# Loading two of 336 expert slabs by eight-partition transfers on eight DMA engines

## The chip, the cores and the metric

One core of one Trainium2 chip runs the kernel. The metric is the time of one execution on the device in microseconds. What reads as "the clock" below is the share of TensorE's full clock that was granted.

## What is computed

The reference is a trunk of two layers on 256 tokens of width 1024, with a memory of 256 rows. Each layer has a mixer (stick-breaking attention, chunked gated linear attention and cross attention to the memory, each gated and summed). The first layer then has a dense SwiGLU block, the second a mixture of experts:

```python
def moe_swiglu(h, w_router, w_gate_up, w_down):
    t = h.reshape(-1, dm)
    top_val, top_idx = lax.top_k((t @ w_router), TOP_K)          # 2 of 8 experts
    top_w = jax.nn.softmax(top_val, axis=-1)
    combine = jnp.sum(jax.nn.one_hot(top_idx, N_EXPERTS) * top_w[..., None], axis=1)
    for e in range(N_EXPERTS):
        y = y + combine[:, e:e + 1] * swiglu(t, w_gate_up[e], w_down[e])
```

An expert's weights are 1024 x 7168 (gate and up) and 3584 x 1024 (down), in float32. All eight experts are used, so 352 MB of expert weights pass through the core in one execution.

## The kernel before

The mixers and the dense block run first, to about 735 us. The change touches only what comes after: the mixture of experts, and how its weights are loaded.

**Slots and slabs.** The experts are worked on in slots, one expert a slot and eight of them here (an expert with too many tokens would get a slot more). A slot takes 96 tokens in three blocks of 32, or 64 in two blocks; `BLOCKS_AT` (line 80) gives the first seven as 3, 2, 3, 2, 3, 3, 2, and the eighth has two. An expert's weights come as 42 slabs of 128 partitions x 2048 floats, 1 MB each (`EXP_SLABS`, line 57), 336 slabs in all. On the host they are laid out as `moe_slabs[expert, j // 3, partition, j % 3, :]`, so that three slabs in a row are 24 KB of contiguous memory in each partition (`expert_slabs_in_order`, line 2388). Inside a slot PE works the slabs off in order: gate and up of 1024 hidden columns, the next gate and up, then the down product of the columns before, and so on. The last six slabs (36 to 41) are down products, with the gathering of the next slot's tokens between slabs 37 and 38.

**Buffers.** `exp_raw` (line 234) holds 21 slabs; slab j of a slot from the third one on lies in place j % 21. The first two slots use one more buffer, exp_extra, and load each slab by a transfer of its own (`single_slabs`, line 592). From the third slot on, `expert_slabs` (line 603) loads slabs 0 to 38 of a slot by 13 transfers of three slabs (line 610), and slabs 39, 40 and 41 by single ones (line 616). All are issued by SP, in the order of use. Before each one SP waits for `slab_used`, which PE raises after its last matmul on a slab, so that a place is free before it is loaded again. SP's program has the third slot written out and the others as a loop over i, from 3 to the number of slots (lines 648 to 652). The number of the expert is read from a table at each slot.

**Waits of PE.** `wait_slab` (line 372): PE waits for `more_ready` at each third slab and for one of three `end_ready` semaphores at each of the last three. A landed transfer adds 16. PE, ScalarE and VectorE have slots 0 to 6 written out, and then a loop.

Of the kernel before, what the change touches and what calls it, by code (L numbers as in the profile page):

```python
# [13 lines left out]
P = 128  # L14
# [10 lines left out]
D_FF, EXPERTS, D_EXP = 2816, 8, 3584  # L25
# [15 lines left out]
EXP_RAW, LOAD = 21, 3  # L41
FIRST_RAW = EXP_RAW + 1
SINGLE_SLOTS = 2
DGE_SCRATCH = 4096


# [10 lines left out]
EXP_SLABS = sum(GU) + sum(DN)  # L57
SINGLE = SINGLE_SLOTS * EXP_SLABS
HT = DM // P
# [20 lines left out]
BLOCKS_AT = (3, 2, 3, 2, 3, 3, 2)  # L80
# [87 lines left out]
def trunk(nc, x_in, mem_in, mix_norm_g, w_in, sb_q_g, sb_k_g, gla_a_up, gla_a_b, gla_o_g, ca_q_g,  # L168
# [10 lines left out]
    with ExitStack() as ctx:  # L179
        def sb(name, shape, dt=F32):  # L180
            return ctx.enter_context(nc.sbuf_tensor(name, shape, dt))

        def sem(name):
            return ctx.enter_context(nc.semaphore(name))
# [14 lines left out]
        slot_i = sb("slot_i", [1, 1 + EXPERTS + OVER], I32)  # L199
# [34 lines left out]
        exp_raw = sb("exp_raw", [P, EXP_RAW, EXP_SLAB])  # L234
# [121 lines left out]
        more_ready = [sem(f"more_ready{i}") for i in range(EXP_RAW // LOAD)]  # L356
        end_ready = [sem(f"end_ready{i}") for i in range(LOAD)]

        END = EXP_SLABS - LOAD

        def load_ready(i, j):

            if j % EXP_RAW == END % EXP_RAW:
                return i * 16
            return i * (16 * EXP_SLABS // EXP_RAW) + 16 * (j // EXP_RAW)

        def place(i, j):

            n = i * EXP_SLABS + j if type(i) is int else SINGLE
            return n % FIRST_RAW if n < SINGLE else j % EXP_RAW  # L370

        def wait_slab(pe, i, j):

            if type(i) is int and i * EXP_SLABS + j < SINGLE:
                pe.wait_ge(first_ready[place(i, j)], 16 * ((i * EXP_SLABS + j) // FIRST_RAW + 1))
            elif j >= END:
                pe.wait_ge(end_ready[j - END], i * 16 + 16)
            elif j % LOAD == 0:
                pe.wait_ge(more_ready[j % EXP_RAW // LOAD], load_ready(i, j))
# [176 lines left out]
        def _(sp):  # L556
# [35 lines left out]
            def single_slabs(e, i, js):  # L592
                for j in js:
                    sp.wait_ge(slab_used, i * EXP_SLABS + (PRE + j + 1 - FIRST_RAW))
                    sp.dma_start(exp_slots[place(i, j)], moe_slabs[bass.ds(e, 1), j // LOAD, :, j % LOAD, :]
                                 .rearrange("e p n -> (e p) n"))\
                        .then_inc(first_ready[place(i, j)], 16)

            def last_holder(j):

                return max(n for n in range(SINGLE) if n % FIRST_RAW == j)

            def expert_slabs(e, i):
                for j in range(0, END, LOAD):
                    if type(i) is int and j < EXP_RAW:
                        sp.wait_ge(slab_used, PRE + 1 + max(last_holder(j + n) for n in range(LOAD)))
                    else:
                        sp.wait_ge(slab_used, i * EXP_SLABS + (PRE + j + LOAD - EXP_RAW))
                    n = j % EXP_RAW
                    sp.dma_start(exp_raw[:, n:n + LOAD, :].rearrange("p a n -> p (a n)"),  # L610
                                 moe_slabs[bass.ds(e, 1), j // LOAD]
                                 .rearrange("e p a n -> (e p) (a n)"))\
                        .then_inc(more_ready[n // LOAD], 16)
                for j in range(END, EXP_SLABS):
                    sp.wait_ge(slab_used, i * EXP_SLABS + (PRE + j + 1 - EXP_RAW))
                    sp.dma_start(exp_slots[j % EXP_RAW], moe_slabs[bass.ds(e, 1), j // LOAD, :, j % LOAD, :]
                                 .rearrange("e p n -> (e p) n"))\
                        .then_inc(end_ready[j - END], 16)

# [19 lines left out]
            for n in range(EXP_RAW // LOAD):  # L639
                sp.sem_inc(more_ready[n], load_ready(SINGLE_SLOTS, n * LOAD) - 16)  # L640
            for n in range(LOAD):
                sp.sem_inc(end_ready[n], SINGLE_SLOTS * 16)
            single_slabs(0, 0, range(FIRST_RAW, EXP_SLABS))
            sp.wait_ge(r_table, 1)
            slots = sp.value_load(slot_i[0:1, 0:1], min_val=EXPERTS, max_val=SLOTS)
            e = sp.value_load(slot_i[0:1, 2:3], min_val=0, max_val=EXPERTS - 1)
            single_slabs(e, 1, range(EXP_SLABS))
            e = sp.value_load(slot_i[0:1, 3:4], min_val=0, max_val=EXPERTS - 1)
            expert_slabs(e, SINGLE_SLOTS)
            with sp.Fori(SINGLE_SLOTS + 1, slots) as i:  # L650
                e = sp.value_load(slot_i[0:1, bass.ds(i + 1, 1)], min_val=0, max_val=EXPERTS - 1)
                expert_slabs(e, i)
            for t in range(NT):
# [1165 lines left out]
        def _(pe):  # L1819
# [478 lines left out]
            def expert(i, blocks, blocks_ago, blocks_next):  # L2298
                j = 0

                def gate_and_up(s, part):
                    nonlocal j
                    w = 2 * lanes_wide(s)
                    n = KT // GU[s]
                    for q in part:
                        wait_slab(pe, i, j)
                        for kk in range(n):
                            k = q * n + kk
                            if is_first(i) and (s, k) == (0, KT // 2):
                                pe.wait_ge(x_dve, 1)  # L2310
                            for b in range(blocks):
                                for g in range(LANES):
                                    c = kk * LANES * w + g * w
                                    ins = mm(lane(pa, g)[:, b * BW:b * BW + w],
                                             xf[:, k, b * LANE:(b + 1) * LANE],
                                             exp_slots[place(i, j)][:, c:c + w],
                                             k == 0, k == KT - 1)
                        ins.then_inc(slab_used, 1)
                        j += 1

                def down(s, part):
                    nonlocal j
                    pe.wait_ge(e_turned, i * STEPS + (s + 1))
                    chunks = hidden_chunks(s)
                    n = EXP_SLAB // DM
                    for q in part:
                        wait_slab(pe, i, j)
                        for kk in range(n):
                            k = q * n + kk
                            for b in range(blocks):  # L2330
                                for g in range(LANES):
                                    c = kk * DM + g * OUT
                                    ins = mm(lane(ps, g)[:, b * OUT:(b + 1) * OUT],
                                             hf[:, s % 2, (b * chunks + k) * LANE:
                                                (b * chunks + k + 1) * LANE],
                                             exp_slots[place(i, j)][:, c:c + OUT],
                                             s == 0 and k == 0 and b * OUT % BW == 0,
                                             s == STEPS - 1 and k == HT_END - 1)
                        ins.then_inc(slab_used, 1)
                        j += 1  # L2340
# [101 lines left out]
```

## Time and profile before

| what | value |
|---|---|
| median of 3 runs | 1557.95 us (1557.13 to 1558.28) |
| the profiled execution | 1556.87 us |
| its span, first to last instruction | 1555.1 us |
| granted TensorE clock | 0.995 |
| PE, VectorE, ScalarE, GpSimd busy | 97%, 35%, 28%, 5% |
| moved by DMA | 480.50 MB, mean 309 GB/s |

The span is the time between the first and the last instruction of the profiled execution; the 1.8 us between it and the time of that execution lie around it. Busy shares are means over the whole span. The DMA share is the mean over the core's sixteen DMA engines, so that a share of one half can mean sixteen engines at half their time or eight engines at all of theirs. A number behind `x` is a count.

### The profile page before, as it was taken

What the parts mean: (1) busy time and instruction counts of PE and PEld (TensorE: products, weight loads), DVE (VectorE), ACT (ScalarE), POOL (GpSimd) and SP (SyncE); (2) the same over time, 40 slices, a digit from 0 to 9 for tenths busy, and PEclk for the clock granted to TensorE, in tenths of its full rate; (3) what the DMA queues carried; (4) which work ended last, traced back from release to release, by engine and by line L of the source; (5) the groups of instructions that cost most, each with busy time, mean ns of one, the idle gap of its engine ahead of it and who ended that gap; (6) DMA issues with size and microseconds to landing.
All of it is one profiled execution on the core that took longest, in us unless ns stands there. A gap on an engine that the chain in (4) does not pass through costs nothing.

```text
span 1555.1 us, 33054 instructions
## 1 busy us (share of the span) xinstructions
PE 1505.2 (97%) x15014; PEld 972.0 (63%) x15014; DVE 544.1 (35%) x638; ACT 439.9 (28%) x566; POOL 81.1 (5%) x117
## 2 busy tenths in 40 slices
PE   8999999999999999999999999999999999999876
PEld 6888888788888887888335353354543553545324
DVE  5755575655567664666200101001010010010100
ACT  5557654544445657453000000000000000000000
POOL 5211100000002111000000000000000000000000
PEclk9999999999999999999999999999999999999999
DMA  7555454665655654777999999999999999999995
GB/s 274 178 155 169 141 172 155 224 189 175 204 177 177 189 151 149 247 274 278 420 421 392 415 427 428 425 430 427 427 428 428 428 427 427 414 418 425 428 429 220
DMA packets 86361, 480.50 MB, mean 309 GB/s; under 512 B 10384, under 2 KB 12496, under 8 KB 63184
## 3 DMA queue, kind: packets, MB, share of 16 engines
q1 hardware_dynamic: 84592, 474.67, 78.6%
q0 software_dynamic: 1632, 3.74, 0.8%
q8 instruction: 118, 1.93, 0.5%
q14 instruction: 19, 0.16, 0.0%
HBM read 477.34 MB, written 1.05 MB: 308 GB/s over the span
## 4 chain that ended last, share of the span: by engine, by line
PE 87%; DMA 7%; DVE 2%; POOL 2%; issue 1%; ACT 0%; SPq 0%; DVEq 0%; POOLq 0%
PE pa L2045 28%; PE ps L2045 20%; PE pa L1916 13%; PE pa L1918 12%; PE pa L1917 12%; DMA exp_raw<-in_moe_slabs 6%; DVE w_lo L1240 1%; DMA w_raw<-in_w_mem_kv 1%; POOL hrs L763 1%; POOL head_gains L692 0%; PE ps L1843 0%; PE ps L2218 0%; PE ps L2039 0%; DVE hs L1788 0%; PE pa L1951 0%
## 5 line engine op out<-in xcount | busy, mean ns | idle before, releaser
L2045 PE MATMUL pa<-exp_raw,xf 128*32 128x512 f32 (+1 forms) x5064 | 490.8, 542 | 15.9 <-DMA exp_raw<-in_moe_slabs 12.8
L2045 PEld LDWEIGHTS pa<-exp_raw,xf 128*32 128x32 f32 x5064 | 176.2, 110 | 306.1 <-issue 232.8
L1240 DVE TENSOR_TENSOR w_lo<-w_raw,w_hi 128x1024 fp32r<-128x1024 f32 x226 | 274.2, 1231 | 121.9 <-ACT w_hi L876 113.0
L876 ACT ACTIVATE w_hi<-w_raw 128x1024 fp32r<-128x1024 f32 (+1 forms) x228 | 236.9, 1053 | 148.6 <-PE pa L1918 147.2
L2045 PE MATMUL ps<-exp_raw,hf 128*32 128x256 f32 x4480 | 251.8, 379 | 14.6 <-issue 8.4
L1916 PE MATMUL pa<-w_hi,r 128*128 128x512 f32 x600 | 240.5, 401 | 1.9 <-DVE r L1275 1.8
L1917 PE MATMUL pa<-w_lo,r 128*128 128x512 f32 x600 | 234.6, 391 | 0.0
L1918 PE MATMUL pa<-w_hi,r 128*128 128x512 f32 x600 | 234.5, 391 | 0.0
L2045 PEld LDWEIGHTS ps<-exp_raw,hf 128*32 128x32 f32 x4480 | 152.9, 110 | 112.9 <-issue 22.2
L1788 DVE TENSOR_TENSOR hs<-pa,hs 128x768 f32<-128x768 f32 (+3 forms) x32 | 23.7, 741 | 569.3 <-ACT hs L1195 569.3
L1195 ACT ACTIVATE hs<-pa 128x768 f32<-128x768 f32 (+3 forms) x32 | 20.4, 637 | 588.7 <-PE pa L2045 588.7
L1916 PEld LDWEIGHTS pa<-w_hi,r 128*128 128x128 f32 x600 | 112.9, 188 | 29.4 <-issue 3.2
L1918 PEld LDWEIGHTS pa<-w_hi,r 128*128 128x128 f32 x600 | 113.0, 188 | 24.4
L1917 PEld LDWEIGHTS pa<-w_lo,r 128*128 128x128 f32 x600 | 113.2, 189 | 22.1
L1916 PE MATMUL pa<-w_hi,xt 128*128 128x512 f32 (+1 forms) x320 | 123.3, 385 | 2.9 <-DVE xt L1275 2.7
L1918 PE MATMUL pa<-w_hi,xt 128*128 128x512 f32 (+1 forms) x320 | 121.3, 379 | 0.0
L1917 PE MATMUL pa<-w_lo,xt 128*128 128x512 f32 (+1 forms) x320 | 121.3, 379 | 0.0
L1916 PEld LDWEIGHTS pa<-w_hi,xt 128*128 128x128 f32 x320 | 60.2, 188 | 16.0 <-issue 2.7
L1918 PEld LDWEIGHTS pa<-w_hi,xt 128*128 128x128 f32 x320 | 60.2, 188 | 11.5
L1917 PEld LDWEIGHTS pa<-w_lo,xt 128*128 128x128 f32 x320 | 60.2, 188 | 10.6
L1773 DVE TENSOR_TENSOR yf<-ps,yf 128x768 fp32r<-128x768 f32 (+1 forms) x7 | 5.9, 843 | 75.9 <-ACT yf L1182 75.9
L1182 ACT ACTIVATE yf<-ps 128x768 fp32r<-128x768 f32 (+1 forms) x7 | 5.0, 719 | 82.7 <-PE ps L2045 82.7
(266 smaller groups left out, 831.6 us busy)
## 6 DMA issues: line engine op xcount, KB each, us to landing
exp_raw<-in_moe_slabs SPq DMA_DIRECT2D x78, 3072.0 KB, 28.7
exp_raw<-in_moe_slabs SPq DMA_DIRECT2D x99, 1024.0 KB, 10.0
w_raw<-in_w_in SPq DMA_DIRECT2D x104, 512.0 KB, 4.4
w_raw<-in_ff_w_gate_up SPq DMA_DIRECT2D x44, 512.0 KB, 4.6
w_raw<-in_ff_w_down SPq DMA_DIRECT2D x22, 512.0 KB, 4.2
w_raw<-in_w_mem_kv SPq DMA_DIRECT2D x16, 512.0 KB, 5.6
w_raw<-in_w_out SPq DMA_DIRECT2D x16, 512.0 KB, 4.4
w_raw<-in_w_br_sb SPq DMA_DIRECT2D x8, 512.0 KB, 3.8
```

The source lines that it names most:

```text
L763: pool.tensor_tensor(dst[:, 0:n], src[:, 0:n], half[:, 0:n], ALU.pow)\
L876: act.activation(dst, raw, ACT.Copy).then_inc(hi_ready, 1)
L1182: act.activation(yf[:, 0, 0:blocks * OUT], ps[:, 0:blocks * OUT], ACT.Copy)\
L1195: act.activation(hidden_rows(s, blocks), gate_up(s, 0, blocks), ACT.Silu)\
L1240: dve.tensor_tensor(dst, raw, hi.bitcast(F32), ALU.subtract)\
L1773: dve.tensor_tensor(yf[:, 1, 0:blocks * OUT], ps[:, 0:blocks * OUT], yf[:, 0, 0:blocks * OUT].bitcast(F32), ALU.subtract)\
L1788: dve.tensor_tensor(hidden_rows(s, blocks), gate_up(s, 1, blocks), hidden_rows(s, blocks), ALU.mult).then_inc(e_h, 1)
L1916: pe.matmul(dst, hi, m_hi, start=first, stop=False)
L1917: pe.matmul(dst, hi, m_lo, start=False, stop=False)
L1918: return pe.matmul(dst, lo, m_hi, start=False, stop=last)
L2045: return pe.matmul(dst, a, b, start=start, stop=stop, skip_group_check=True)
```

## The change

In the slots with i = 3 and i = 5 (`LOW_SLOTS`), slab 41, the last one, is no longer loaded by one transfer of 128 partitions. It is loaded by sixteen transfers of eight partitions each, with 8 KB a partition. `LOW_SETS` lists them: for k = 0 to 3 and a = 0 to 3, the partitions 32k + a, 32k + a + 4, ... up to 32k + a + 28. Each adds 16 to a semaphore of their own, `low_ready`, and PE waits for 256 of it a set. As these slots no longer raise `end_ready[2]`, the later waits on that semaphore are lower by 16 for each such slot before. To tell the slots apart, SP's loop is written out for slots 2 to 6 (`range(SINGLE_SLOTS, len(BLOCKS_AT))`) and remains a loop from slot 7 on. The first condition in `expert_slabs` gains `i == SINGLE_SLOTS`, so that only the third slot takes its waits from the buffers' first holders, as before.

```diff
--- before.py
+++ after.py
@@ -41,6 +41,8 @@
 EXP_RAW, LOAD = 21, 3
 FIRST_RAW = EXP_RAW + 1
 SINGLE_SLOTS = 2
+LOW_SLOTS = (3, 5)
+LOW_ROWS, LOW_STEP = 8, 4
 DGE_SCRATCH = 4096
 
 
@@ -356,7 +358,16 @@
         more_ready = [sem(f"more_ready{i}") for i in range(EXP_RAW // LOAD)]
         end_ready = [sem(f"end_ready{i}") for i in range(LOAD)]
 
+        low_ready = sem("low_ready")
+
         END = EXP_SLABS - LOAD
+        LAST = EXP_SLABS - 1
+        LOW_SETS = [slice(32 * k + a, 32 * (k + 1), LOW_STEP)
+                    for k in range(P // 32) for a in range(LOW_STEP)]
+
+        def low_before(i):
+
+            return sum(n < i for n in LOW_SLOTS) if type(i) is int else len(LOW_SLOTS)
 
         def load_ready(i, j):
 
@@ -373,6 +384,10 @@
 
             if type(i) is int and i * EXP_SLABS + j < SINGLE:
                 pe.wait_ge(first_ready[place(i, j)], 16 * ((i * EXP_SLABS + j) // FIRST_RAW + 1))
+            elif j == LAST and type(i) is int and i in LOW_SLOTS:
+                pe.wait_ge(low_ready, 16 * len(LOW_SETS) * (low_before(i) + 1))
+            elif j == LAST:
+                pe.wait_ge(end_ready[j - END], i * 16 + 16 * (1 - low_before(i)))
             elif j >= END:
                 pe.wait_ge(end_ready[j - END], i * 16 + 16)
             elif j % LOAD == 0:
@@ -602,7 +617,7 @@
 
             def expert_slabs(e, i):
                 for j in range(0, END, LOAD):
-                    if type(i) is int and j < EXP_RAW:
+                    if type(i) is int and i == SINGLE_SLOTS and j < EXP_RAW:
                         sp.wait_ge(slab_used, PRE + 1 + max(last_holder(j + n) for n in range(LOAD)))
                     else:
                         sp.wait_ge(slab_used, i * EXP_SLABS + (PRE + j + LOAD - EXP_RAW))
@@ -613,6 +628,13 @@
                         .then_inc(more_ready[n // LOAD], 16)
                 for j in range(END, EXP_SLABS):
                     sp.wait_ge(slab_used, i * EXP_SLABS + (PRE + j + 1 - EXP_RAW))
+                    if j == LAST and type(i) is int and i in LOW_SLOTS:
+                        for rows in LOW_SETS:
+                            sp.dma_start(exp_raw[rows, j % EXP_RAW, :],
+                                         moe_slabs[bass.ds(e, 1), j // LOAD, rows, j % LOAD, :]
+                                         .rearrange("e p n -> (e p) n"))\
+                                .then_inc(low_ready, 16)
+                        continue
                     sp.dma_start(exp_slots[j % EXP_RAW], moe_slabs[bass.ds(e, 1), j // LOAD, :, j % LOAD, :]
                                  .rearrange("e p n -> (e p) n"))\
                         .then_inc(end_ready[j - END], 16)
@@ -645,9 +667,10 @@
             slots = sp.value_load(slot_i[0:1, 0:1], min_val=EXPERTS, max_val=SLOTS)
             e = sp.value_load(slot_i[0:1, 2:3], min_val=0, max_val=EXPERTS - 1)
             single_slabs(e, 1, range(EXP_SLABS))
-            e = sp.value_load(slot_i[0:1, 3:4], min_val=0, max_val=EXPERTS - 1)
-            expert_slabs(e, SINGLE_SLOTS)
-            with sp.Fori(SINGLE_SLOTS + 1, slots) as i:
+            for i in range(SINGLE_SLOTS, len(BLOCKS_AT)):
+                e = sp.value_load(slot_i[0:1, i + 1:i + 2], min_val=0, max_val=EXPERTS - 1)
+                expert_slabs(e, i)
+            with sp.Fori(len(BLOCKS_AT), slots) as i:
                 e = sp.value_load(slot_i[0:1, bass.ds(i + 1, 1)], min_val=0, max_val=EXPERTS - 1)
                 expert_slabs(e, i)
             for t in range(NT):
```

## Rows read from the trace of the kernel before

**Rows 1.** The page: span, busy time, and the DMA of the 40 slices.

```profile
span 1555.1 us, 33054 instructions
...
PE 1505.2 (97%) x15014; PEld 972.0 (63%) x15014; DVE 544.1 (35%) x638; ACT 439.9 (28%) x566; POOL 81.1 (5%) x117
...
DMA  7555454665655654777999999999999999999995
GB/s 274 178 155 169 141 172 155 224 189 175 204 177 177 189 151 149 247 274 278 420 421 392 415 427 428 425 430 427 427 428 428 428 427 427 414 418 425 428 429 220
```

**Rows 2.** Busy time by stretch: the fourth to the eighth slot, one line each.

```profile
core 0: us, PE busy (x) PEld busy (x) DVE busy (x) ACT busy (x) POOL busy (x), PEclk, DMA share, GB/s
...
1046.00:1126.00 80.00, 79.06 (x1197) 38.38 (x1193) 9.40 (x14) 4.07 (x7) 0.00 (x0) 1.00 1.00 427
1126.00:1243.00 117.00, 113.93 (x1645) 56.59 (x1641) 11.00 (x14) 4.82 (x7) 0.00 (x0) 1.00 1.01 428
1243.00:1359.00 116.00, 114.02 (x1670) 56.62 (x1665) 11.13 (x14) 4.92 (x7) 0.00 (x0) 1.00 1.00 423
1359.00:1435.00 76.00, 75.13 (x1105) 34.89 (x1094) 8.85 (x13) 3.97 (x7) 0.00 (x0) 1.00 0.99 420
1435.00:1548.00 113.00, 90.48 (x1320) 42.13 (x1319) 9.43 (x15) 4.31 (x8) 0.00 (x0) 0.97 0.88 375
```

**Rows 3.** The waits from 1440 us to the end, on DMA, of the matmuls.

```profile
engine line waited for: us in total, times, longest us
...
PE pa L2045 <- DMA exp_raw<-in_moe_slabs: 12.8, 10, 2.6
...
PE ps L2045 <- DMA exp_raw<-in_moe_slabs: 6.2, 3, 2.3
```

**Rows 4.** The chain of waits from 1420 us on.

```profile
1429.30 4.89 PE ps L2045 x152
...
1438.33 43.15 DMA exp_raw<-in_moe_slabs
...
1487.10 46.35 DMA exp_raw<-in_moe_slabs
...
1533.58 4.79 PE ps L2045 x145
...
1539.61 7.82 PE ps L2045 x174
...
1547.44 0.61 ACT hs L1214
```

**Rows 5.** The DMA view from 1521 to 1545 us, 40 slices of 0.6 us.

```profile
DMA  9899999999997674344444545564532110000001
GB/s 410 369 437 410 382 492 410 382 492 382 410 464 300 287 300 205 164 178 191 191 191 205 218 205 218 218 232 191 205 164 96 68 27 0 0 0 0 0 0 27
DMA packets 547, 5.47 MB, mean 228 GB/s; under 512 B 69, under 2 KB 69, under 8 KB 69
```

**Rows 6.** The DMA view from 1354 to 1374 us, 40 slices of 0.5 us.

```profile
DMA  8997955592698999999969997794995999997996
GB/s 344 442 393 344 393 246 246 197 639 98 295 442 344 475 393 492 442 393 393 541 295 492 393 393 246 295 328 197 393 393 246 393 492 393 393 442 344 492 492 295
DMA packets 337, 7.48 MB, mean 374 GB/s; under 512 B 32, under 2 KB 32, under 8 KB 32
...
exp_raw<-in_moe_slabs SPq DMA_DIRECT2D x3, 3072.0 KB, 20.7
```

**Rows 7.** The DMA view from 720 to 1540 us, the queue that loads code.

```profile
q8 instruction: 88, 1.44, 0.7%
```

**Rows 8.** The DMA view of 1375 to 1528 and 870 to 905 us; issues of the page.

```profile
DMA packets 3417, 65.41 MB, mean 428 GB/s; under 512 B 381, under 2 KB 381, under 8 KB 381
...
DMA packets 2021, 14.75 MB, mean 422 GB/s; under 512 B 223, under 2 KB 223, under 8 KB 223
...
exp_raw<-in_moe_slabs SPq DMA_DIRECT2D x13, 1024.0 KB, 15.0
...
exp_raw<-in_moe_slabs SPq DMA_DIRECT2D x78, 3072.0 KB, 28.7
...
w_raw<-in_w_in SPq DMA_DIRECT2D x2, 64.0 KB, 2.5
```

**Rows 9.** SP in order of time, and what line 616 issues.

```profile
936.35 0.85 SPq L610 DMA_DIRECT2D exp_raw<-in_moe_slabs  x2
...
1087.69 3.78 SPq L616 DMA_DIRECT2D exp_raw<-in_moe_slabs  x3
1096.29 0.34 SPq L610 DMA_DIRECT2D exp_raw<-in_moe_slabs  x1
...
1301.33 5.50 SPq L616 DMA_DIRECT2D exp_raw<-in_moe_slabs  x3
1314.23 0.34 SPq L610 DMA_DIRECT2D exp_raw<-in_moe_slabs  x1
...
L616 SPq DMA_DIRECT2D exp_raw<-in_moe_slabs x18: 332/333/333, 988.8 to 1494.4; - x18
...
DMA to landing us min/median/max: 23.6/31.4/46.4
```

## The prediction

> **What bounds the kernel now.** I read the page first, for the slices [rows 1]: from the twentieth slice on, TensorE and the DMA engines are both nearly full, the DMA at 414 to 430 GB/s in most slices. That is the expert stage, which begins near 735 us. Busy shares don't say which of the two sets the end, so the stage was cut into its slots [rows 2]. In the wide slots (three blocks of tokens) PE is busy for 114 of 116 or 117 us. In the last slot it is busy for 90 of 113 us, while the DMA share is 0.88 with the idle end of the slot counted in. The waits of that last slot [rows 3] say whose fault that is: PE's matmuls wait 13 times for exp_raw, 12.8 + 6.2 = 19.0 us in all. The chain of waits [rows 4] agrees. It runs along PE until 1438 us, then through two loads that take 43.15 and 46.35 us from issue to landing, then through 14 us of PE work on what came with the last of them, and 8 us of tail. A 3 MB load at 428 GB/s takes 7.35 us by itself. So the rest of 46 us is time in the queue, and what sets the end is how early the whole queue is worked off.
>
> **The queue has two halves.** The DMA view of the last 24 us of transfers [rows 5] is what this case turns on. Every load was issued long before (the answer has no issue in it). The rate is above 360 GB/s until 1528.2, has fallen to 205 at 1530.0, stays between 164 and 232 until 1538.4, and ends at 1540.8. Half of 428 is 214: eight of the sixteen engines finish near 1530, the other eight near 1540. The lagging eight hold up each load, since a load has landed when its last engine is done. The opposite view is the dip at 1354 to 1374 [rows 6], where SP issues late, because PE in the wide slots frees buffers more slowly than the DMA fills them. The rate averages 374 against 428 there, with a trough of 197 to 246 about 1357.5: again about half. The leading eight have run dry, and the lagging ones haven't. The missing (428 - 374)/428 x 20 = 2.5 us of all sixteen engines is about 5 us of eight.
>
> Why eight lag isn't shown directly. The likeliest source is code loading: 88 packets of queue q8 from 720 to 1540 us hold 0.7% of 16 x 820 us, 92 us in all, 1.04 us each [rows 7]. Dealt out to eight engines alone these make 11.5 us per engine, near the 10 us of the gap. Dealt out to sixteen they would make no gap.
>
> **The change, part by part.**
>
> 1. Two slabs move to the "low" eight engines. A slab is 1.05 MB, at 428 GB/s [rows 8] 2.45 us of all sixteen engines. Each of the 16 new transfers has eight partitions and I take it to run on eight engines, one row of 8 KB each. So the eight engines that don't take part save 2.45 us per slab, 4.9 us for two, and the others spend 4.9 us more. If the lagging eight are the spared ones, their end goes from 1540.8 to 1535.9. The leading eight go from 1530.0 to at most 1534.9, and to about 1531 if the idle 5 us of the dip are used up by the added work. Either way the lagging ones still end last, and the last big load lands 4.9 us earlier: 1533.4 becomes 1528.5.
>
> 2. Is the saving kept across the dip? The lagging engines must not run dry at 1357 to 1372, or PE's pace takes the 4.9 us back. The three loads issued there land 20.7 us after issue (median) [rows 6]. Less 7.35 us of their own and the 2.5 us that a 64 KB load needs from issue to landing [rows 8], 10.8 us were spent behind earlier loads on the slowest engine. That is more than 4.9, so the saving is kept.
>
> 3. PE must be able to take it. The 19.0 us of waits [rows 3] lie between 1444 and 1533.6, so PE could have been ready for the last big load at 1514.6. It needs 4.9 us of that. After the landing the same 14 us of PE work follow. The very last slab is needed at the end of these, and it lands earlier by the same amount.
>
> 4. SP issues 16 transfers where it issued one. Back to back, issues are 0.52 us apart (two end within 0.85 us and the second takes 0.33) [rows 9], so a set costs 16 x 0.52 = 8.3 us in place of 0.5. In the fourth slot the set would end at 1091.1 + 8.3 = 1099.4, and the next slot's first load was issued at 1096.3: 3.1 us late. In the sixth it ends at 1306.5 + 8.3 = 1314.8 against 1314.2. Single loads of line 616 take 23.6 us at the least to land [rows 9], so 20 us of transfers stand before them, and a load issued 3 us late leaves no hole. I cost it at zero; without that queue it would cost up to 3.1 + 0.6 us. POOL's queue isn't passed.
>
> 5. Small transfers: no row has an eight-partition load. From below, single-slab loads at 422 GB/s against 428 for mostly triple ones [rows 8] make a slab 2.48 us against 2.45, so two thirds of a boundary cost at most 0.03 us and sixteen cost 0.8 us per set, on engines with a surplus of some 4 us: nothing. From above, if each waited for the landing of the one before at 2.5 us, a set would hold the low engines for 40 us, and two sets would end them some 60 us later than now. Loads are seen to overlap (28.7 us to land, one each 7.35), so I take the lower end.
>
> 6. SP's loop over slots 3 to 6 becomes straight code, and one group of waits is replaced by constants. SP sits waiting for most of each slot, so its instructions are hidden. If its code takes three more 16 KB packets, that is 3 us on one engine at worst, 0.4 us dealt out to eight. Below nothing is possible too, since a loop may have its code loaded again each time. PE's new wait on low_ready replaces its wait on end_ready, one for one. Behind it are the last two down products' matmuls, and the low engines were ahead when the slab was due.
>
> Sum: -4.9 us, with -5.3 to -4.5 from point 6. The profiled execution took 1556.87 us (span 1555.1 and 1.8 around it), 0.07% under the median of 1557.95. Off the median it makes 1553.0.
>
> **The rivals.**
>
> *The other eight's partitions are the bottleneck (no gain).* Half the rows of each set lie in partitions 64 to 127. If whole loads write these by the other eight engines, then for that half of a set, 64 KB an engine, two engines write where one did, at 27 GB/s each. If the place written to can take no more than 27 GB/s, then the lagging engines share it for as long as they were meant to save: 2.45 saved, 2.45 lost, and the end stays at 1557.95 (1557 to 1558.7). For it: each engine runs at a flat 428/16 = 26.8 GB/s, which could be the engine's limit or that of where it writes. Against it: nothing, since no row shows two engines on one group of partitions. The Trainium skill, "SBUF — State Buffer", section "Door 1: The DMA port swizzle", speaks for this rival: it says that a transfer's rate goes by how many of 16 ports its partitions reach, that each takes about 27 GB/s, and that partitions 64 to 127 lie behind eight ports of their own. By that rule the time is 1557.95, and by the rows alone either is possible.
>
> *The spared eight are the leading ones (slower).* No row tells which engines lag, so the sign of point 1 rests on the guess that code loading and the eight-row transfers use different halves. If they use the same half, it gets 4.9 us more instead of 4.9 us less: 1540.8 becomes 1545.7 and the time 1562.9. It decides in the last slot, at each PE wait. The Trainium skill, "DMA: Bandwidth & Descriptors", section on why a DMA increments its semaphore by 16, says that such a transfer takes the lowest-numbered engines, but neither it nor a row tells where code loading goes.
>
> *A part is lost.* The two writers share for part of the time, or the low engines get late through small transfers: a gain of 0.5 to 3, near 1556.
>
> *It doesn't do what it says.* An eight-row transfer spread over all sixteen engines would change nothing. It falls to the no-gain case.
>
> **How the numbers follow.** Full gain 0.50, no gain 0.28 with the undone split in it, part gain 0.10, slower 0.12. A difference of 0.2%, 3.1 us, is about what a measurement of this kernel can tell from none. Full gain is faster (0.50), and a third of the part gains are (0.03). The same: 0.28 + 0.07 and little else. Slower: 0.12. The prediction is the likeliest case's, 1553.0, whose own range is 1551.5 to 1554.2 (its sum's 0.4 us either way, and the 0.8 us by which the lowest of the runs shown lies under their median). The stated range goes from 1551.5 over the part gain and the no-gain case to 1559.0, which leaves out the slower case and some noise.
>
> **What would show it.** In the last 24 us of transfers the plateau near 214 GB/s would shrink from 8 to at most 5 us, and the final load's slowest engine would end near 1536. The dip at 1357 would be shallower, since the leading engines are no longer dry. Line 610's last load would land near 1528.5, and PE's waits on exp_raw would sum to about 14 us instead of 19. The waits in slots 4 to 6 would stay at none. For the rival of shared partitions: packets of the lagging engines lengthen beside each set, and the plateau at the end shrinks only because the leading engines come later. For the slower one: the plateau grows to some 18 us. The forecast is wrong if PE waits on the new semaphore, if SP's issue of a set exceeds the 20 us of queued work, or if the rate falls below 400 GB/s around 1122 or 1338, where the sets should land (31.4 us after issue by the median of line 616 [rows 9]).

## The result, and the profile after

| | median | range | runs |
|---|---|---|---|
| before | 1558.12 us | 1557.13 to 1558.41 | 4 |
| changed | 1572.91 us | 1571.44 to 1574.01 | 4 |

The ratio is 1.009, with a 95% interval from 1.0079 to 1.0102: 14.8 us slower. I had forecast 4.9 us less. The profiled execution of the changed kernel took 14.6 us more of span than that of the kernel before, so its trace shows the whole of the loss.

The page of the changed kernel, lines as in [rows 1]:

```profile
span 1569.7 us, 33069 instructions
...
PE 1511.1 (96%) x15014; PEld 973.8 (62%) x15014; DVE 544.2 (35%) x638; ACT 439.9 (28%) x566; POOL 81.0 (5%) x117
...
DMA  8555454666655554777999999999999999999994
GB/s 273 180 156 160 148 175 160 212 191 189 188 173 190 160 175 144 273 279 286 419 414 390 421 428 428 427 426 428 363 428 429 426 429 388 387 428 425 429 430 186
```

TensorE is as busy as before (1511 against 1505 us). The slices show where the DMA rate gave way: 363 GB/s in the twenty-ninth slice and 388 and 387 in the thirty-fourth and thirty-fifth, where [rows 1] have nothing below 414 from the twenty-third slice to the thirty-ninth. The bytes are the same.

The first of these dips, in the DMA view of the changed kernel from 1112 to 1132 us, 40 slices of 0.5 us. The set of the fourth slot is worked off there:

```profile
DMA  9797999999799989947962989998935991499599
GB/s 442 311 508 328 475 377 426 377 246 229 147 213 246 229 180 262 377 131 180 492 180 98 590 344 442 508 360 180 426 66 115 229 426 33 98 295 393 246 541 377
DMA packets 611, 6.06 MB, mean 303 GB/s; under 512 B 168, under 2 KB 168, under 8 KB 168
```

The engines' share stays at nine tenths while the rate falls to 303 GB/s in the mean, and to between 147 and 262 for the four microseconds from 1116. So nothing was missing from the queue: sixteen busy engines moved half as much. Where engines run dry, as in [rows 6], the share falls with the rate.

The end of the transfers, to be held against [rows 5] (40 slices of 0.75 us, from 1530 us):

```profile
DMA  9799999999997897754554310112111112100000
GB/s 426 328 470 371 459 404 426 415 393 415 426 448 317 360 426 295 284 251 197 240 229 186 131 44 33 44 66 66 55 55 55 55 44 87 44 0 0 0 22 0
DMA packets 593, 6.42 MB, mean 214 GB/s; under 512 B 74, under 2 KB 74, under 8 KB 74
```

The rate falls to between 186 and 284 from 1542 to 1546.5, and then stays between 33 and 87 from 1547 to 1556. One engine moves 428/16 = 27 GB/s. The second plateau is two engines, alone for 9 us or so. In [rows 5] there was a single plateau, of eight.

The landings say the same. Each of sixteen engines adds to a load's semaphore as it finishes, and the trace has the times. These are those of the very last slab, the first landing in us and then all sixteen after it:

```
before   1528.85   0.0 0.0 0.1 0.1 0.3 1.4 1.5 1.7 | 10.5 10.6 10.8 10.8 11.1 11.6 11.8 12.0
changed  1539.98   0.0 0.0 2.2 2.3 2.4 3.1 3.8 5.3 |  6.4  6.5  7.4  7.6  7.8  8.2 16.8 16.9
```

Eight lead and eight lag before, as I had read from the plateau. After it, two stand 8.7 us behind all others. The last landing went from 1540.85 to 1556.88, 16.0 us later.

The chain of waits of the changed kernel, first around the first set and then from 1400 us on, as in [rows 4]:

```profile
1106.08 31.80 DMA exp_raw<-in_moe_slabs
...
1138.01 20.84 PE pa L2068 x192
```

```profile
1407.46 38.14 DMA exp_raw<-in_moe_slabs
...
1455.12 43.17 DMA exp_raw<-in_moe_slabs
...
1503.91 45.55 DMA exp_raw<-in_moe_slabs
1549.60 12.39 PE ps L2068 x320
1562.01 0.60 ACT hs L1237
```

The fifth slot's first load was issued at 1106.08 and landed at 1137.87. PE starts that slot at 1138.01, where it started it at 1131.92 before. The end is the old pattern, loads of 38 to 46 us in the queue (three of them in the chain where [rows 4] have two), 16 us later: the last big one lands at 1549.46 instead of 1533.44, and has 12.4 us of PE work behind it. In the view of waits PE's matmuls wait for exp_raw for 24.8 us, where [rows 3] have 19.0:

```profile
PE pa L2068 <- DMA exp_raw<-in_moe_slabs: 16.7, 11, 2.0
...
PE ps L2068 <- DMA exp_raw<-in_moe_slabs: 8.1, 5, 2.0
```

Four of these waits, 6.3 us, lie before 1445 us, in slots where there were none.

Last, SP in order of time around the first set, and its sixteen transfers (line 633) in the view of that line, as in [rows 9]:

```profile
1087.92 2.06 SPq L638 DMA_DIRECT2D exp_raw<-in_moe_slabs  x2
1091.36 13.41 SPq L633 DMA_DIRECT2D exp_raw<-in_moe_slabs  x16
1106.08 2.51 SPq L625 DMA_DIRECT2D exp_raw<-in_moe_slabs  x3
```

```profile
L633 SPq DMA_DIRECT2D exp_raw<-in_moe_slabs x32: 627/644/841, 1091.4 to 1325.2; - x32
```

An issue of eight partitions takes 644 ns and they come 0.84 us apart (13.41 us for 16). I had counted 0.52. The next load was issued at 1106.1 instead of 1096.3.

### The profile page after: what moved, and what is told of

Same layout as the page of the kernel before. It is cut to its first block, busy times and chain, and to the rows that moved or that the text cites. A ratio compares the mean times of both kernels' runs of the same rounds, so it can differ in the third digit from the quotient of the medians.

```text
span 1569.7 us, 33069 instructions
## 1 busy us (share of the span) xinstructions
PE 1511.1 (96%) x15014; PEld 973.8 (62%) x15014; DVE 544.2 (35%) x638; ACT 439.9 (28%) x566; POOL 81.0 (5%) x117
## 4 chain that ended last, share of the span: by engine, by line
PE 82%; DMA 11%; DVE 2%; POOL 2%; issue 1%; SPq 1%; ACT 0%; DVEq 0%; POOLq 0%
PE pa L2068 25%; PE ps L2068 18%; PE pa L1939 12%; PE pa L1941 12%; PE pa L1940 12%; DMA exp_raw<-in_moe_slabs 10%; DVE w_lo L1263 1%; DMA w_raw<-in_w_mem_kv 1%; SPq L633 1%; POOL hrs L786 1%; POOL head_gains L715 0%; PE ps L1866 0%; PE ps L2241 0%; PE ps L2062 0%; DVE hs L1811 0%
## 5 line engine op out<-in xcount | busy, mean ns | idle before, releaser
L2068 PE MATMUL ps<-exp_raw,hf 128*32 128x256 f32 x4480 | 257.4, 385 | 16.1 <-DMA exp_raw<-in_moe_slabs 8.1
L2068 PE MATMUL ps<-sel,hn 128*32 128x64 f32 (+1 forms) x1152 | 24.9, 245 | 6.0 <-issue 6.0
```

The lines of the kernel that those rows point to most:

```text
L2068: return pe.matmul(dst, a, b, start=start, stop=stop, skip_group_check=True)
```

## The experiments

Three things could have made the loss: the sixteen issues (theory B), the small transfers as such (theory D), or where they write (theory A). Theory A is the rival that I had priced at no gain: two engines that write to the same group of partitions halve each other. Theory C is all the rest of the change. The edits are against the changed kernel, last_six's against the kernel before; `...` stands for what is left out. Times are medians in us, against the kernel before on the same chip.

| run | time | kernel before beside it | ratio (95%) |
|---|---|---|---|
| whole_alone | 1558.6 | 1558.38 | 1.0004 (0.9994 to 1.0014) |
| issue_alone | 1561.63 | 1558.38 | 1.0021 (1.0011 to 1.0031) |
| half_own | 1555.33 | 1558.38 | 0.9989 (0.9980 to 0.9999) |
| half_other | 1567.1 | 1558.38 | 1.0058 (1.0041 to 1.0075) |
| extra_small | 1559.08 | 1558.2 | 1.0006 (0.9997 to 1.0015) |
| extra_own | 1562.14 | 1558.2 | 1.0026 (1.0017 to 1.0036) |
| extra_other | 1572.06 | 1558.2 | 1.0099 (1.0084 to 1.0115) |
| last_six | 1556.54 | 1558.2 | 0.9990 (0.9981 to 0.9999) |
| first_only | 1564.83 | 1557.97 | 1.0042 (1.0028 to 1.0057) |
| extra_four | 1558.06 | 1557.97 | 1.0001 (0.9991 to 1.0011) |
| upper_whole | 1570.34 | 1557.97 | 1.0076 (1.0059 to 1.0093) |
| extra_four_other | 1563.04 | 1558.19 | 1.0032 (1.0020 to 1.0043) |

### What is left when the sets are whole, and what the issues cost

whole_alone:

```diff
-        LOW_SETS = [slice(32 * k + a, 32 * (k + 1), LOW_STEP)
-                    for k in range(P // 32) for a in range(LOW_STEP)]
+        LOW_SETS = [slice(0, P)]
```

> The changed kernel, but each of the two sets is one transfer of 128 partitions: what is left of the change is SP's straight code, the new semaphore and the later constants. Theory A (the eight-partition transfers themselves cost the time, by writing to partitions that other engines are writing to): within 1 us of the kernel before. Theory B (SP's sixteen issues hold the queue up): the same, within 1 us. Theory C (the straight code or the changed waits cost): +15 us, as the changed kernel.

It measured +0.2 us. The straight code of SP, the new semaphore and the later constants cost nothing: theory C is out, and the whole loss is in the sets.

issue_alone:

```diff
+                        sp.dma_start(exp_raw[:, j % EXP_RAW, 0:EXP_SLAB - 128],
+                                     moe_slabs[..., 0:EXP_SLAB - 128]...).then_inc(low_ready, 16)
                         for rows in LOW_SETS:
-                            sp.dma_start(exp_raw[rows, j % EXP_RAW, :], ...
+                            sp.dma_start(exp_raw[rows, j % EXP_RAW, EXP_SLAB - 128:], ...
```

PE's wait on `low_ready` is raised to the seventeen transfers of a set.

> The changed kernel with the bytes of the sets put back on all sixteen engines: one transfer of 128 partitions for columns 0 to 1919, and sixteen of eight partitions for the last 128 columns, 512 bytes a row. SP issues seventeen transfers a set (14 us at 0.84 us each). Theory A: within 1.5 us of the kernel before. Theory B: at least two thirds of the loss, +10 us or more.

Measured +3.2 us (one of the ten executions took 3126 us and is not in the ratio). SP in order of time shows that the issues are all there:

```profile
1094.10 13.40 SPq L637 DMA_DIRECT2D exp_raw<-in_moe_slabs  x16
1108.81 5.95 SPq L625 DMA_DIRECT2D exp_raw<-in_moe_slabs  x3
```

The sixteen take 13.40 us and the next load is issued at 1108.8, later than in the changed kernel, and yet four fifths of the loss are gone. Theory B is out as the main cause. The 3.2 us are more than theory A allowed (1.5). The landings of the very last slab put them on engines and not on the queue: fourteen shares are there within 10.4 us of the first, and the last two at 13.2 and 13.8. A late issue isn't felt by two engines alone, so the short rows of 512 bytes are the likelier source, on the two lagging engines that take them (theory E below). Yet the sixteen packets that an engine gets of a set take 27 ns each, 0.4 us in all, and why they cost more than that no run shows.

### Where the transfers write

half_own and half_other load half of each set's rows and leave out the others, so the last slab of two slots is partly that of an earlier one:

```diff
         LOW_SETS = [slice(32 * k + a, 32 * (k + 1), LOW_STEP)
-                    for k in range(P // 32) for a in range(LOW_STEP)]
+                    for k in range(2) for a in range(LOW_STEP)]       # half_own
+                    for k in range(2, 4) for a in range(LOW_STEP)]    # half_other
```

> The changed kernel without the eight transfers of each set that go to partitions 64 to 127; these rows of the two slabs are not loaded at all. Eight transfers a set are left, all to partitions 0 to 63. Theory A: the packets keep their 310 ns, no engine is slowed, and the time is that of the kernel before or up to 5 us less (-5 to +1 us). Theory B: half the issues, so at least a third of the loss: +4 to +7 us. Theory D (any eight-partition transfer runs slowly): +7 us.

> The changed kernel without the eight transfers of each set that go to partitions 0 to 63; these rows are not loaded at all. Bytes, number of transfers and issues are those of half_own, only the partitions differ. Theory A: packets of 8 KB take 620 ns and those of 24 KB up to 1900 ns while a set is worked off, and the time is 5 us or more over half_own. Theories B and D: the time of half_own, within 1 us.

They have the same bytes, the same number of transfers and the same number of issues. The medians are 11.8 us apart: -3.1 us for partitions 0 to 63, and +8.7 us for 64 to 127. The DMA views of 1112 to 1132 us, first half_own, then half_other:

```profile
DMA  9999899999997959997996939498989959296989
GB/s 426 508 377 459 311 393 410 442 508 410 410 508 311 590 246 623 377 475 279 492 557 295 639 147 688 197 590 344 475 344 442 541 246 688 98 688 295 541 344 442
DMA packets 627, 8.58 MB, mean 429 GB/s; under 512 B 121, under 2 KB 121, under 8 KB 121
```

```profile
DMA  9897949999987999899779989897999859669699
GB/s 459 377 492 295 623 197 557 229 246 197 246 164 164 197 262 262 197 262 295 229 311 492 475 344 524 279 524 246 459 279 475 180 115 459 213 246 508 262 492 426
DMA packets 570, 6.63 MB, mean 331 GB/s; under 512 B 112, under 2 KB 112, under 8 KB 112
```

The mean is 429 GB/s against 331. In the second one the rate is between 164 and 262 from 1115.5 to 1121, with the engines as busy as in the first. The durations of the single packets in the trace, 1100 to 1400 us, name the size of the effect. A packet of 8 KB takes 309 to 320 ns when nothing disturbs it, one of 24 KB 912:

```
kernel            8 KB packets of 500 to 700 ns    24 KB packets of 1800 ns and more
before               0 of 1152                          6
whole_alone          0 of 1152                          9
half_own             0 of 1024                          2
extra_own            0 of 1280                          1
extra_four           0 of 1216                          2
changed            250 of 1152                         52
half_other         190 of 1024                         41
extra_other        235 of 1280                         43
extra_four_other   183 of 1216                         16
```

The doubled packets are in each kernel of the table that sends eight or four rows to partitions 64 to 127, and in none that sends them to 0 to 63 alone. The Trainium skill, "SBUF — State Buffer", section "Door 1: The DMA port swizzle", states the rule: a port takes about 27 GB/s, and partitions 64 to 127 have eight ports of their own. These runs agree that the two halves of the partitions are apart, with some 620 to 650 ns for 8 KB where two engines share. How far the slowing reaches is another matter, to which extra_four_other comes back.

### Which engines the transfers take

The landing times of half_own's first set show six of its eight shares done at 1117.5 us and the other two at 1123.0, where the eight leading engines are within 1.7 us of each other. Those of its very last slab show the same two: eight shares within 1.6 us, six from 8.1 to 9.7 and two at 13.1 and 13.3. The six are the lagging engines that were spared, by this reading, and they end at 1536.6 us, 4.3 before the 1540.85 of [rows 5], where point 1 had 4.9. So the saving exists as long as nobody writes to partitions 64 to 127. That made theory E: of the eight engines of an eight-partition transfer two are among those that lag. To test it without taking anything away, whole_alone got eight needless transfers behind each of the two slabs, into exp_extra, which is free after the second slot:

```diff
+                        if low_before(i):
+                            sp.wait_ge(extra_ready, 16 * 8 * low_before(i))
+                        for k in (0, 1):                    # extra_other: (2, 3)
+                            for a in range(LOW_STEP):
+                                rows = slice(32 * k + a, 32 * (k + 1), LOW_STEP)
+                                sp.dma_start(exp_extra[rows, 0:2048],      # extra_small: 0:128
+                                             moe_slabs[..., rows, j % LOAD, 0:2048]...)\
+                                    .then_inc(extra_ready, 16)
```

> The kernel before in its loads (each set one transfer of 128 partitions), with eight needless transfers of eight partitions x 512 bytes behind each of the two slabs, to a buffer that is free by then, in partitions 0 to 63. The control for the next two: SP's issues without their bytes. Every theory: +0 to +1.5 us against the kernel before.

> As extra_small, with whole rows of 8 KB: eight rows more for each engine that the eight-partition transfers use, to partitions 0 to 63. Theory E (two of those eight engines are among the eight that lag, as the landing times of the changed kernel and of half_own suggest): the two lagging ones get 8 x 0.31 = 2.5 us more per slot, so the end comes 5 us later, +4 to +6 us over extra_small. Theory F (all eight are engines that lead, as my prediction had it): they have 10 us to spare, so the time of extra_small within 1 us.

> As extra_own, but the same eight transfers go to partitions 64 to 127. Theory A with E: their packets take 620 ns instead of 310, so the two lagging engines get 5 us more per slot, 10 us in all, and the spared engines behind the same partitions lose 2.5 us per slot: +9 to +12 us over extra_small. Theory A with F: the spared laggards lose 2.5 us per slot, +5 us. Without theory A: the time of extra_own.

extra_small is the control, with +0.9 us. extra_own is 3.1 us over it: less than E's 4 to 6, and outside F's 1. (The eight lagging shares of extra_small's last slab spread from 11.5 to 13.3 us, so a part of the 5 us can be used up before the two are the last.) The DMA view of extra_own from 1535 us on (slices of 0.625 us) decides:

```profile
DMA  5444555521111210000100000000000799930000
GB/s 236 197 197 197 210 210 210 210 118 66 52 52 52 79 52 13 0 0 0 26 0 0 0 0 0 0 0 0 0 0 0 308 413 393 413 151 0 0 0 0
```

After the plateau of eight there is one at 52 to 79 GB/s, two engines, from 1541.2 to 1544.4. In the landings of its last slab the last two are at 15.6 and 15.7 us, and the next one at 12.1. My own forecast gave all eight engines 10 us to spare. Two of them had none.

extra_other is 13.0 us over the control, a little over the 9 to 12 expected. The same bytes in the other half of the partitions cost 9.9 us more than in extra_own.

extra_four and extra_four_other ask which part of the loss needs those two engines:

```diff
-                                rows = slice(32 * k + a, 32 * (k + 1), LOW_STEP)
+                                rows = slice(32 * k + a, 32 * k + 16, LOW_STEP)
```

> extra_own with transfers of four partitions instead of eight: the engines that a transfer of four takes get the same eight rows more, to places of their own. If the lagging two of the eight are among those four: the time of extra_own, +3 to +5 us over extra_small, and the two last landing times stand apart as they do there. If both are among the other four: extra_small's time within 1 us. One in each: +2 to +5, with one engine apart.

> extra_four with its four-partition transfers sent to partitions 64 to 127 instead of 0 to 63. The four engines they take have time to spare (extra_four cost nothing), so what is left is what sharing does to others. Theory A: each lagging engine that regularly writes to those partitions is at half its rate while 64 KB pass beside it, 2.5 us a slot, 5 us in all, +4 to +6 us over extra_four. If the loss needs the two lagging engines themselves in the set: extra_four's time within 1 us.

With transfers of four partitions the same rows per engine cost +0.1 us against the kernel before. So both lagging engines are among the four of the eight that a four-partition transfer doesn't take, and the four that it takes have the 5 us to spare. Sent to partitions 64 to 127, the same transfers cost 4.85 us (4.8 us over extra_four's, within 4 to 6), though no engine that lacks time carries a byte of them. The DMA views from 1116 to 1130 us, first extra_four, then extra_four_other:

```profile
GB/s 328 398 398 421 398 468 445 515 375 328 515 375 562 421 421 468 375 421 445 398 492 421 398 655 234 492 492 351 492 351 492 492 281 632 328 351 562 281 492 421
DMA packets 503, 6.01 MB, mean 430 GB/s; under 512 B 79, under 2 KB 79, under 8 KB 79
```

```profile
GB/s 445 492 351 187 187 211 211 257 117 304 140 304 117 281 304 187 328 328 445 351 468 398 468 421 304 585 492 328 492 421 562 421 281 562 351 492 492 281 538 421
DMA packets 416, 5.01 MB, mean 358 GB/s; under 512 B 72, under 2 KB 72, under 8 KB 72
```

430 GB/s against 358. An engine that has nothing to do with a transfer loses about 2.5 us per 64 KB that each taking engine writes beside it. That is the size that theory A gave.

But it isn't theory A alone, and this I had not looked for. If the engines of an ordinary load each write to a place of their own, theory A has four engines write to the places of four others, so eight of sixteen run at half their rate and the whole would fall to 321 GB/s. In the fourteen slices from 1117.05 to 1121.95 it is 224, half of 428. The landings show who lost. Below are the last 3 MB load of the sixth slot and the first of the seventh, with the second set between them: by how much each share lies further behind than 14.75 us, which is what the leading shares take in the kernel before. Shares are in their order of landing.

```
                   the eight that land first                the other eight
before             0.0 0.0 0.0 0.0 0.0 0.0 0.0 0.0 | 0.0 0.0 1.0 0.9 0.5 0.4 0.2 0.0
extra_own          0.0 0.0 2.5 2.5 2.5 2.6 2.6 2.6 | 0.0 0.1 0.5 0.2 0.0 0.5 4.1 4.0
extra_four         0.0 0.0 0.0 0.0 2.6 2.6 2.5 2.5 | 0.0 0.1 0.6 1.0 0.8 0.3 0.1 0.0
extra_four_other   2.7 2.9 2.7 2.8 5.4 5.2 5.2 5.2 | 3.2 3.4 3.6 3.5 2.6 2.2 2.4 1.5
```

extra_own's row is theory E once more: six leading shares and two lagging ones take its 2.5 us (the two show 4.0 and 4.1, and no run splits off the rest; lagging shares slip by up to 1.0 us in the kernel before too). In extra_four only the four takers are later. In extra_four_other the takers lose 5.2 us, as theory A has it, but all the other twelve lose time too, 1.5 to 3.6 us, and the four leading ones of them 2.7 to 2.9. So four engines that write to partitions 64 to 127 hold up all sixteen. Whether that happens at the places written to or on the way there, no run tells.

### One set, and a transfer of 64 partitions

first_only is `LOW_SLOTS = (3,)`.

> The changed kernel with the set in the fourth slot alone; the sixth loads its last slab whole. Theory A with E: each set puts 16 rows on the two lagging engines where 8 were, half of them at 620 ns, so a set costs some 5 us there and what sharing costs on top; one of two gives half the loss, +6 to +9 us against the kernel before. If PE's pace in the wide slots swallowed the first set's cost: 0 to +2. If the first set's late start of the fifth slot carried all of it: +13 or more.

+6.9 us, 46% of the loss. PE's pace in the wide slots swallows next to nothing, and the two sets add up.

upper_whole keeps the eight transfers to partitions 0 to 63 and loads the rest by one of 64 partitions:

```diff
-                    for k in range(P // 32) for a in range(LOW_STEP)]
+                    for k in range(2) for a in range(LOW_STEP)] + [slice(P // 2, P)]
```

> The changed kernel with partitions 64 to 127 of each set loaded by one ordinary transfer of 64 partitions in place of eight transfers of eight. Theory A (two engines writing to the same partitions' place halve each other, whichever transfer does it): sixteen engines now send four rows each to where eight write, at 620 ns a row, 2.5 us for all; the two lagging ones get eight rows of 0.31 and four of 0.62 us for eight of 0.31 before: +2.5 us a set, +4 to +6 in all. Without sharing of places: they get 1.2 us more a set, +1 to +3.

+12.4 us, twice what I expected and nearly as bad as the changed kernel (+14.8), with seven fewer issues a set. In its trace 81 packets of 8 KB take more than 700 ns from 1100 to 1400 us, up to 1065, where the other kernels have four to six such packets. That is three times 310, as if three engines shared a place. Which three, no run shows, and the size stays unexplained.

### A version that beats both

The last chain starts from a 3 MB load with 14 us of PE work behind it. last_six loads slabs 36 to 41 singly in each slot instead of 39 to 41, without the change:

```diff
-        end_ready = [sem(f"end_ready{i}") for i in range(LOAD)]
-        END = EXP_SLABS - LOAD
+        end_ready = [sem(f"end_ready{i}") for i in range(2 * LOAD)]
+        END = EXP_SLABS - 2 * LOAD
-            if j % EXP_RAW == END % EXP_RAW:
+            if j % EXP_RAW >= END % EXP_RAW:
...
```

> A candidate to beat both: the kernel before with the last six slabs of a slot (36 to 41) loaded singly, not the last three. The chain of waits ends in a 3 MB load whose landing starts 14 us of PE work; its first slab is there 2 x 2.45 us earlier if it is a transfer of its own. The tail is bound by the lagging engines either way. If the tail's wait is what sets the end: -4 to -5 us. If the time is bound elsewhere (by the bytes alone, or by the very last slab): 0.

Measured -1.7 us by the medians, ratio 0.9990 (0.9981 to 0.9999): faster than the kernel before by about 0.1%, which is below the 0.2% that I had called the limit of what can be told, and a third of what I expected. The changed kernel's ratio is 1.009, so the two are some 16 us apart. Its profiled execution has the span of the kernel before, 1555.1 us. Its chain of waits:

```profile
1481.59 45.58 DMA exp_raw<-in_moe_slabs
...
1527.21 5.39 PE pa L2045 x96
1532.60 4.56 PE ps L2045 x143
1537.16 0.55 issue
1537.71 5.18 PE ps L2045 x126
1542.89 1.21 issue
1544.10 3.23 PE ps L2045 x51
...
1547.35 0.61 ACT hs L1214
```

The wait has moved as meant: the work now hangs on a load that lands at 1527.16, and the products of slabs 36 and 37 start at 1532.6 without a wait, where [rows 4] start them at 1533.58. But then there are 0.55 and 1.21 us in which PE waited for nothing that the profile shows, and the last slab landed at 1543.69, 2.8 us later than before and 0.41 us before the second pause ends. ScalarE's last step starts at 1547.35, against 1547.44. The tail seems to have had two ends close to each other, of which only one was taken away.

## Why the prediction was wrong, point by point

**The reading of before held.** Eight engines lead and eight lag by 10 us, and what the lagging ones finish is what sets the end: the landing times show it. That code loading makes them lag was only argued, but the trace of before bears it out. From the load that first lands at 1108.1 us to the one at 1356.8, the eight leading shares keep their distances to 0.1 us, while the lags of the other eight grow from 46.6 to 92.4 us in sum. They grow step by step, while 29 packets of the code queue pass: 1.6 us a packet. A packet itself takes 1.0 to 1.1 us, and why the lag is more isn't shown. No run changed the code loads.

**Point 1 failed, and it failed twice.** "The eight engines that don't take part save 2.45 us per slab" is what half the set took back. I had this as the rival *the other eight's partitions are the bottleneck*, gave it 0.28, and preferred the full gain although nothing in the rows spoke against the rival. half_own and half_other show the doubling, and extra_four_other its price, some 2.5 us per 64 KB. The rival had a spared lagging engine save 2.45 us and lose as much. It lost more: of the sixteen shares of the very last slab fourteen land at 1542.2 us or later, where the rival would have the six spared lagging ones as before, at 1539.3 to 1540.85.

The rival's own price was wrong too, since it and I both took the eight engines of the set for the eight that lead. In the set are two of those that lag. Such an engine has 16 rows for 8: eight at 0.31 and eight at about 0.63 us, 7.5 us for 2.5. That is 5.0 us a set and 10 us for both, out of the 14.8. I had made the question of which eight an all-or-nothing one, all lagging engines spared or none, and priced the second at +4.9 us. The mixed case with sharing wasn't among the rivals, and lies outside the range. For the 4.8 us that remain extra_four_other has the likeliest source. There engines that share no place lost 1.5 to 3.6 us too, so the two lagging ones would lose another 2.5 us or so a set, while the leading ones write to the upper half. That makes 7.5 us a set (2.5 for the rows, 2.5 for their doubling, 2.5 for the rest) and 15 us for both, an estimate, where the last landing came 16.0 us later. The same sum holds for extra_other, where 13.0 us were measured. Theory A alone gave 10 us for either.

**Point 2, the dip,** was to say whether a saving is kept. There was none to keep.

**Point 3:** PE's part held in reverse. The last big load came 16.0 us later, and the time rose by 14.8: it had 12.4 us of PE work behind it instead of 13.8, most of the difference being the pause of 1.24 us between the last two pieces of PE in [rows 4].

**Point 4** was mis-sized: an issue of eight partitions takes 0.84 us and not 0.52, a set 13.4 us and not 8.3, and the next load was 9.8 us late instead of 3.1. The mechanism (a queue of 20 us hides it) was right: with all the issues in place, issue_alone lost 3.2 us at most, and on two engines alone.

**Point 5:** in their own places small transfers with rows of 8 KB run at full rate, 309 to 320 ns a row, as I took it. The upper bound of 2.5 us each was far off. What I hadn't bounded is a row written to another engine's place.

**Point 6** held: whole_alone is 0.2 us from the kernel before.

**The signs that I had named** were good ones. Of the rival I wrote that packets of the lagging engines would lengthen beside each set, and that the forecast is wrong if the rate falls below 400 GB/s near 1122: it fell to 303. The predicted shrinking of the plateau did happen, from eight engines for 8 us to eight for some 4, but two engines stayed behind it. The waits in slots 4 to 6, which were to stay at none, came to four, 6.3 us in all, before 1445 us.

## What to carry to other kernels

A load has as many limits as it has engines and places to write to: before bytes are moved from slow engines to quick ones, ask which partitions the quick ones will write to and who else is writing there, since the engines beside them are slowed without a byte of theirs. When a whole class of engines is to be relieved, find out engine by engine who is in it: a class that is three quarters right here put the extra work on the two that set the end. A needless transfer into a free buffer, once to each half of the partitions, with a tiny one as the control, puts both questions to the chip, and a fall of the rate at full DMA share is the sign of sharing in the profile.

## What the runs showed of the hardware

- While engines of eight- or four-partition transfers write to partitions 64 to 127 beside ordinary loads, many packets of 8 KB take some 630 ns (medians of 622 to 633 in the kernels above) and some of 24 KB 1840 to 1940, where they take 310 and 912 undisturbed. Four such engines are enough to bring all sixteen to half their rate (224 GB/s of 428, for 4.9 us).
- A transfer of eight partitions lands in eight shares, and one of 128 in sixteen. SP takes 644 ns to issue the one and 333 ns to issue the other. One of 64 partitions takes 531 to 538 ns, and one of four 597 to 603.
- From 1115 to 1370 us the packets of the code queue, 16 KB each, set eight engines back by some 1.6 us a packet, taken together, and the other eight not at all.
- Of the eight engines that an eight-partition transfer takes six lead and two lag here, and the two aren't among the four of a four-partition transfer.
- One transfer of 64 partitions to the upper half, beside ordinary ones, stretched packets to as much as 1065 ns.
